# A two-block transformer step in float32 on one core: gates and return projection as seven token-major products, weight sums on GpSimd, last experts' blocks in halves

## What is computed

```python
# first block, cut to what matters; u_lat is the modulated input, 256 x 1024
q, k, v, g, glu, gates = split(u_lat @ w_in + b_in)          # g and gates: 2048 columns each
o = retention_in_both_directions(q, k, v, context)           # 256 x 2048, 8 heads
ret = silu(g) * head_norm(o)
y_a = ret @ w_ret_out                                        # 2048 -> 1024
z = depthwise_conv_31_taps(za * sigmoid(zb)) + b
z = silu(layernorm(z) * conv_g + conv_b)
y_b = z @ w_conv_out + b_conv_out
ga, gb = split(sigmoid(gates))
mix = (ga * y_a + gb * y_b) @ w_mix_out + b_mix_out
h = layernorm(ALPHA * h + gt_m * mix)
y = sum over 32 experts of combine[:, e] * ((silu(t @ w_gate[e]) * (t @ w_up[e])) @ w_down[e])
```

## Time and profile before

| | |
|---|---|
| median of three runs | 1438.39 us |
| the profiled execution | 1437.52 us, span 1435.7 us |
| TensorE (PE) busy | 1390.8 us, 97% |
| DVE busy | 611.6 us, 43% |
| ACT busy | 224.4 us, 16% |
| GpSimd busy | 18.1 us, 1% |
| read from HBM | 419 MB, mean 295 GB/s |
| granted TensorE clock, mean | 0.995 |

### The profile page before, as it was taken

How to read it: one execution, slowest core, us unless ns; L and a number is a source line. 1 busy time by engine, 2 the same in 40 slices (tenths; PEclk the granted TensorE clock), 3 DMA queues, 4 the chain that set the end, 5 groups by cost and what they waited for, 6 DMA issues and landing times.

```text
span 1435.7 us, 21518 instructions
## 1 busy us (share of the span) xinstructions
PE 1390.8 (97%) x9242; PEld 981.6 (68%) x9242; DVE 611.6 (43%) x1267; ACT 224.4 (16%) x445; POOL 18.1 (1%) x44
## 2 busy tenths in 40 slices
PE   9999999999999999999999999898999999999986
PEld 7888888678888887555545544444688887565543
DVE  1566899989883147222221122122512326122122
ACT  0211010321201104111011011011211203211001
POOL 0000000000000000000100000000100000000000
PEclk9999999999999999999999999999999999999999
DMA  9735231964344587999999999999443557899995
GB/s 383 317 146 81 81 132 66 350 244 191 128 165 157 211 344 317 398 415 427 409 426 425 426 425 427 425 425 428 157 188 152 219 207 293 311 385 423 426 424 233
DMA packets 36342, 423.05 MB, mean 295 GB/s; under 512 B 4352, under 2 KB 5768, under 8 KB 10776
## 3 DMA queue, kind: packets, MB, share of 16 engines
q1 hardware_dynamic: 33408, 415.33, 70.8%
q10 hardware_dynamic: 1176, 1.84, 1.1%
q0 software_dynamic: 1664, 4.52, 1.0%
HBM read 419.05 MB, written 2.62 MB: 294 GB/s over the span
## 4 chain that ended last, share of the span: by engine, by line
PE 76%; DMA 13%; DVE 9%; issue 1%; SPq 0%; ACT 0%; POOL 0%; DVEq 0%; POOLq 0%
PE PP L1004 21%; PE PP L1356 16%; PE PP L1393 8%; DMA KQ<-in_w_moe 5%; PE MB L1331 5%; DMA ZC<-in_w_moe 4%; PE PP L1160 3%; PE PP L1042 3%; DVE ZC L1698 2%; DMA ring<-in_w_moe 2%; PE PP L1074 2%; PE MB L1134 2%; PE PP L1365 2%; PE PP L1323 2%; DMA ring<-in_w_v 1%
## 5 line engine op out<-in xcount | busy, mean ns | idle before, releaser
L1004 PE MATMUL PP<-uT,ring 128*128 128x256 f32 x704 | 153.5, 379 | 0.0
L1004 PEld LDWEIGHTS PP<-uT,ring 128*128 128x128 f32 x704 | 133.3, 190 | 19.1 <-issue 1.1
L2248 DVE TENSOR_SCALAR wctx<-wctx 128x1 f32<-128x1 f32 x46 | 7.1, 153 | 265.7 <-PE PP L1356 219.6
L1698 DVE SCALAR_TENSOR_TENSOR ZC<-ZC,vec 128x256 f32<-128x256 f32 x240 | 116.2, 484 | 7.8
L1331 PE MATMUL MB<-V 64*128 64x512 f32 x336 | 93.8, 638 | 1.7 <-DVE V L2282 0.9
L1356 PE MATMUL PP<-ring,const 128*64 128x256 f32 x800 | 90.6, 380 | 3.0 <-DMA ring<-in_w_moe 2.9
L1356 PEld LDWEIGHTS PP<-ring,const 128*64 128x64 f32 x800 | 57.7, 137 | 37.8 <-issue 8.6
L2268 DVE SCALAR_TENSOR_TENSOR V<-V,wctx 128x256 f32<-128x256 f32 x84 | 40.7, 485 | 91.4 <-PE MB L1331 71.2
L824 ACT ACTIVATE V<-PP 128x256 f32<-128x256 f32 x42 | 16.2, 385 | 304.8 <-PE PP L1356 283.2
L1393 PE MATMUL PP<-ring,const 128*64 128x512 f32 x272 | 62.1, 598 | 0.0
L2282 DVE TENSOR_TENSOR V<-PP,uT 128x512 f32<-128x512 f32 x32 | 22.1, 692 | 82.3 <-PE PP L1393 82.3
(11 more groups left out here) (563 smaller groups left out, 2112.0 us busy)
## 6 DMA issues: line engine op xcount, KB each, us to landing
ring<-in_w_moe SPq DMA_DIRECT2D x51, 2048.0 KB, 16.8
RA<-in_w_moe SPq DMA_DIRECT2D x18, 2048.0 KB, 16.9
ZC<-in_w_moe SPq DMA_DIRECT2D x18, 2048.0 KB, 18.7
Vc<-in_w_moe SPq DMA_DIRECT2D x17, 2048.0 KB, 18.4
KQ<-in_w_moe SPq DMA_DIRECT2D x17, 2048.0 KB, 17.9
extra<-in_w_moe SPq DMA_DIRECT2D x17, 1792.0 KB, 15.0
ring<-in_w_ada SPq DMA_DIRECT2D x12, 2048.0 KB, 10.4
ring<-in_w_gates SPq DMA_DIRECT2D x7, 2048.0 KB, 7.7
```

The lines of the kernel that those rows point to most:

```text
L1004: ins = pe.matmul(out[:, c, :], W[:, k * width + at:k * width + at + P], X[:, k, :], start=k == 0, stop=k == K - 1)
L1698: ins = V_.scalar_tensor_tensor(conv[:, t, :], zpad[:, t, k:k + L], tap, conv[:, t, :], ALU.mult, ALU.add)
```

## The change

- **Gates and ret as seven products.** Gates (4 blocks) and ret (its 2048 x 1024 weight as two pairs of blocks, summed over two halves of the depth) go by the scheme of g, with token-major results: `token_products` (g and gates), `ret_products`. DVE adds the products into rows `gates_t` and `m_rows`.
- **Weight sums on GpSimd.** Of the five sums of a block, four go to GpSimd from the second g block on, two of the first; all ten of a pair of ret blocks too: 50 instructions of 128x1024. They have seven places in turn (`SUM_RING`). DVE keeps the fifth (and three of the first g block).
- **Mixed rows turned.** `cout` becomes a `tm8` job, the gating with gates is done on rows, and two pieces of 8 transposes (`turn_mixed`) bring the result to channel-major before `mix`.
- **Head norm** moves from DVE to ACT (16 instructions of 128x256, `Identity` with scale and bias).
- **Taps in turns.** Two channel tiles are convolved side by side: a tap waits for the one two before it (`own.follow`). Their places are dealt out anew, through g, gates and the first ret pair.
- **Last experts' blocks in halves.** Up comes as its first and last four k pieces, down as the two halves of every 512 columns (pieces of 1 KB a row); TensorE, DVE and the last scatter work by halves.
- **Bays.** The last ret block goes to RA, and the first nine expert blocks are loaded in another order; KQ is free once the mixed rows are turned, not when mix is done.

```diff
-FIRST_MOE0 = (2, 0, 1, 3, 8, 5, 7, 4, 6)
+FIRST_MOE0 = (2, 0, 6, 3, 8, 4, 1, 7, 5)
...
-                       ("k", 2, ["seven"]), ("v", 4, ["seven"]), ("ada", 8, ["ada"]), ("g", 4, ["seven"]), ("gates", 4, ["cm8"]),
-                       ("ret", 4, ["cm16"]), ("cout", 2, ["cm8"]), ("mix", 2, ["cm8"]))),
+                       ("k", 2, ["seven"]), ("v", 4, ["seven"]), ("ada", 8, ["ada"]), ("g", 4, ["seven"]), ("gates", 4, ["seven"]),
+                       ("ret", 4, ["ret"]), ("cout", 2, ["tm8"]), ("mix", 2, ["cm8"]))),
...
+        SUM_RING = [Eqb, Ddec, Pc, Ph, kw, Kc[:, 0:4, :], Kc[:, 4:8, :]]
...
+            def follow(self, ins):
+
+                self.n += 1
+                ins.then_inc(self.sem, 1)
+                self.eng.wait_ge(self.sem, self.n - 1)
...
+            def weight_sum(i, q, j=1):
+
+                w_wait(pool, J["ret", 2 * SEVEN[i][1] + j, 0]["w"] if i >= R7 else seven_job(i)["w"])
+                if G7 + 2 <= i < S7:
+                    seven_wait(pool, i - 2, 6)
+                if i >= S7:
+                    n = ring_place(i, q, j if i >= R7 else 0)
+                    if n >= len(SUM_RING):
+                        seven_wait(pool, *ring_user(n - len(SUM_RING)))
+                    elif n >= 4:
+                        seven_wait(pool, G7 + 2, 6)
+                x, y, op = weight_pair(*quarters(i, j))[q]
+                nc.gpsimd.tensor_tensor(sum_at(i, q, j if i >= R7 else 0), x, y, op).then_inc(pool_made, 1)
...
-                    t, k = step // TAPS, step % TAPS
+                    t, k = 2 * (step // (2 * TAPS)) + step % 2, step % (2 * TAPS) // 2
...
+            def ret_products(i, after_fourth=None):
+
+                for p in range(7):
+                    n = 7 * i + p
+                    pe.wait_ge(seven_kept, n - 3)
+                    for j in range(2):
...
+                        for k in range(4):
+                            ins = pe.matmul(gate_bank(n - 7 * G7), x[:, k, :], y[:, k, :], start=j == 0 and k == 0, stop=j == 1 and k == 3)
...
             for b in range(4):
                 for p in range(7):
-                    add_gate_product(b, p)
+                    add_token_product(G7 + b, p)
                     if p == 1 and b:
                         gate_ret(b - 1)
-                    if p > 1 and b < 3:
-                        add_weights(G7 + b + 1, p - 2)
-                    if p == 3:
-                        normalise(b)
+                    elif p < 6:
+                        taps(2 if p > 1 else 1)
+                    else:
+                        add_weights(G7 + b + 1, 4)
             gate_ret(3)
-            taps(DT * TAPS - tap_at[0])
+            for b in range(4):
+                for p in range(7):
+                    add_token_product(S7 + b, p)
+                    if b >= 2 and p < 5:
+                        ret_token_sum(b - 2, p)
+                    elif p == 6 and b < 3:
+                        add_weights(S7 + b + 1, 4)
+                    else:
+                        taps(2)
+            left = DT * TAPS - tap_at[0]
...
+            job(J["cout", 1, 0], at_half=lambda: turn_mixed(0))
...
                     pe.wait_ge(m["wg_full"], i * 16 + 16)
                     gate_or_up(0, wg, xs).then_inc(m["gate_done"], 1)
-                    pe.wait_ge(m["wu_full"], i * 16 + 16)
-                    gate_or_up(1, wu, xs).then_inc(m["up_done"], 1)
-                    pe.wait_ge(m["y_kept"], k + 1)
+                    up_halves(wu, i * 16 + 16).then_inc(m["up_done"], 1)
+                    pe.wait_ge(m["y_kept"], i * 2 + (WINDOWS[n] + 1))
...
+                    down_half(0, wd).then_inc(m["down_done"], 1)
+                    pe.wait_ge(m["wd_rest"], i * 16 + 16)
+                    down_half(1, wd).then_inc(m["down_done"], 1)
```

More of the change, by code:

```diff
@@ L172, in make_jobs @@
                 if src != "glu" or b == 3:
-                    loads.append(dict(src=src, b=b, bay=bay_of(phase)))
+                    loads.append(dict(src=src, b=b, bay=3 if (src, b) == ("ret", 3) else bay_of(phase)))
         experts(n)
@@ L404, in build @@
                                           "rooted", "u_scaled", "u2_scaled", "res", "gate_ps", "gate_kept")}
-        fin = {k: sem(f"fin_{k}") for k in ("row", "divided", "scaled", "rows")}
+        fin = {k: sem(f"fin_{k}") for k in ("divided", "scaled", "rows")}
         def out_wait(eng):
@@ L441, in seven_job @@
         def seven_job(i):
-            return J[SEVEN[i][0], SEVEN[i][1], 0]
+            src, b = SEVEN[i]
+            return J[src, 2 * b + 1 if src == "ret" else b, 0]
         def seven_wait(eng, i, p):
@@ L530, in last_experts @@
                     for q in range(3):
-                        sp.wait_ge(m[PARTS[q][1]], i + 1)
-                        sp.dma_start(bays[own[q]], s[bass.ds(3 * e + q, 1)].rearrange("a p n -> p (a n)")
-                                     ).then_inc(m[PARTS[q][0]], 16)
+                        sp.wait_ge(m[PARTS[q][2]], i * 2 + 1 if q == 2 else i + 1)
+                        into, block = bays[own[q]], s[bass.ds(3 * e + q, 1)].rearrange("a p n -> p (a n)")
+                        if q == 0:
+                            sp.dma_start(into, block).then_inc(m[PARTS[q][0]], 16)
+                            continue
+                        for half in range(2):
+                            if q == 1:
+                                part = lambda x: x[:, half * 2048:(half + 1) * 2048]
+                            else:
+                                part = lambda x: x.rearrange("p (c h n) -> p c h n", h=2, n=L)[:, :, half, :]
+                            sp.dma_start(part(into), part(block)).then_inc(m[PARTS[q][half]], 16)
             at = [first_of_moe[0]["w"], J["u2", 0, 0]["w"], first_of_moe[1]["w"], len(loads)]
@@ L614, in _, with bias_row @@
             pool.dma_start(outside, a["outside"]).then_inc(b2["ld"], 16)
-            for n in range(8):
+            def bias_row(n):
                 if n >= 2:
@@ L746, in turned_copy @@
                 ins.then_inc(ret_kept, 1)
+            act.wait_ge(var_ready, 2)
             for b in range(4):
+                for h in (2 * b, 2 * b + 1):
+                    for t in range(LT):
+                        o = On[:, t, h * DV:(h + 1) * DV]
+                        nc.scalar.activation(o, o, ACT.Identity, scale=rstd[:, t * HEADS + h:t * HEADS + h + 1], bias=mv[:, t, h, 1:2])
                 act.wait_ge(seven_kept, 7 * (G7 + b + 1))
@@ L753, in _ @@
             for b in range(4):
-                j = J["gates", b, 0]
-                job_wait(act, j)
-                for i in range(4):
-                    ins = nc.scalar.activation(gT[:, 4 * b + i, :], PP[j["pair"]][:, i, :], ACT.Sigmoid,
-                                               bias=col("b_gates", 4 * b + i))
-                ins.then_inc(pair_free[j["pair"]], 1)
+                act.wait_ge(seven_kept, 7 * (S7 + b + 1))
+                gate = gates_t[:, :, 512 * b:512 * (b + 1)]
+                nc.scalar.activation(gate, gate, ACT.Sigmoid).then_inc(g_silu, 1)
             for half in range(2):
@@ L772, in _ @@
                 ln_say(act, ins, out, 1)
+            for half in range(2):
+                act.wait_ge(ret_turned, 5 + half)
+                for q in range(2):
+                    ins = nc.scalar.activation(m_first[:, 4 * half + 2 * q:4 * half + 2 * q + 2, :], MB[2 * half + q][:, :, :], ACT.Copy)
+                ins.then_inc(ret_kept, 1)
             def route_and_experts(n):
@@ L981, in _, with job @@
         def _(pe):
-            def job(j, tiles=None, between=None):
+            def job(j, tiles=None, between=None, at_half=None):
                 w_wait(pe, j["w"])
@@ L1011, in job @@
                 elif kind in ("tm8", "tm8c"):
-                    X = ucT if kind == "tm8c" else uT
+                    X = conv if j["src"] == "cout" else uT
                     for t in range(LT):
+                        if t and at_half is not None:
+                            at_half()
                         for k in range(DT):
@@ L1152, in gate_products @@
                         w_wait(pe, seven_job(i)["w"])
-                    pe.wait_ge(sums_made, sums)
+                    if i == G7 and sums is not None:
+                        pe.wait_ge(sums_made, 5 * G7 + sums)
+                    if p >= 2:
+                        sums_ready(pe, i, y)
+                        y = sum_at(i, y)
                     if n >= 7 * G7 + 4:
@@ L1699, in convolve @@
                     if step < DT * TAPS - 1:
-                        link(ins)
+                        own.follow(ins)
                     else:
@@ L1803, in _ @@
                     else:
[L1804 removed]
+                        taps((2, 2, 2, 2, 2, 4)[i] if (i, p) != (5, 6) else 0)
                 if i in (2, 3):
@@ L1831, in _ @@
                     decay(h + 2)
-                taps(4 if h < 7 else 0)
+                taps(5 if h < 7 else 0)
                 if h:
```

(2 more changed lines are left out.)

324 lines of the change are left out of this document (213 added, 111 removed).

## The result

| | before | after |
|---|---|---|
| median | 1437.93 us (4 runs, 1437.22 to 1441.15) | 1481.86 us (4 runs, 1480.88 to 1482.01) |
| profiled execution, span | 1435.7 us | 1479.1 us |
| busy: PE, DVE, POOL | 1390.8, 611.6, 18.1 us | 1391.2, 687.3, 151.0 us |

The ratio is 1.0298, with a 95% interval of 1.0286 to 1.031: slower by 3%. I had forecast 1421.0, with 1414 to 1460 as range. The prediction was wrong, in sign and in range.

A forecast was written before the change was run, and what follows sets the result against it. TensorE's matmul count bounds g, gates and ret, and the weight stream follows PE's start: gates -6.9, ret -6.9, turns +1.8 (net -12.0) and experts' ends -5.4 give -17.4 us, so 1421.0 us, range 1414 to 1460.

The forecast's parts named there:

- What covers it: In g, gates and ret: GpSimd's sums, DVE's additions and taps, and ACT's head norm cost nothing, hidden beside other work.
- Rival 1: From g to ret, GpSimd sums and DVE taps exclude each other: stage 42 us later, 1463 us; chance 0.22.
- Gates 12.08 us a block, 6.9 us less: Gates: four jobs of 13.81 us become four blocks of 12.08 us, 6.9 us less.
- Ret 6.9 us less: Ret: 4 x 64 = 256 matmuls become 2 x 112, 6.9 us less.
- Turns 1.8 us, cout at nothing: Before mix: two pieces of eight transposes add 1.8 us of PE; token-major cout costs nothing and waits hide.
- A sum on GpSimd 2.45 us: In g, gates and ret: each 1024-element sum takes GpSimd 2.45 us, fifty of them 122 us.
- rival 2: In gates and ret, GpSimd sums are slower than its one row says: 1430 us at 3.0 us each; chance 0.15.
- A pair of taps 0.91 us: DVE in g and gates: two taps taken in turns cost 0.91 us together.
- The 10.7 us for 26 taps of the first ret pair: DVE in the first ret pair: 26 taps take 10.7 us, part of 19.3 of 24.2 us.
- Tails 5.4 us: Last experts' blocks in halves at both experts' ends: 2.7 us less for each, 5.4 in all.
- The last scatter's half beside DVE: At the experts' ends: half of the last scatter is done beside DVE's last part, some 0.5 us.
- The experts' stream moves with PE's start: First block's experts: bays tie the weight stream to PE's start, so the end moves by the same time.

The follow-up runs named there:

- experiments 3 and 5: 3: changed kernel without 91 of its 93 taps, 1433.15 us; 5: all weight sums on DVE, 40 taps earlier, 1443.09 us, then also ret in full, 1428.80 us.
- experiment 1: Kernel before, plus 45 idle GpSimd sums of 1024 elements that nobody needs: 1504.21 us, ratio 1.046.
- experiment 6: Against the run with early taps and ret in full (1428.80 us), GpSimd again makes four of five sums of g and gates blocks: 1428.66 us, ratio 0.9926.

## Why the prediction was wrong

**The step that failed** is "What covers it", with its words "This sum costs three things at nothing, each by work beside it". GpSimd's sums and DVE's taps are not beside each other. I added up each engine apart (10.3 us of GpSimd, 11.5 of DVE, against 13.0), where the sum of those parts of both that exclude each other had to be held against 13.0. Rival 1 did that: 16.8 us for a g block, and 16.8 was measured. The match is in part luck. By its own terms (4 x 2.45 + 1.22 + 1.23 + 9 x 0.485) g comes to 16.6. In the block shown above the four sums took 10.9 us, in which the excluding lengths of both engines add up to 12.5, so the hold-off is a little less than the full lengths; and in the 5.9 us without a sum DVE spent some 2 on additions, which this count leaves out. Rival 1 had a chance of 0.22, "because the rule is only a page's here". What spoke for it (DVE at 88 and 96% by my own count) said how dear it would be if true; what spoke against it was the absence of rows, which is no evidence. As its time lay 42 us away on the wrong side, the range of 1460 also cut off the case.

**Rival 1's own size** was short by 19 us (1463). g is right, gates too (65.6 against 2 x 16.8 and two lighter blocks). The first ret pair was put at 37 us and took 52.2. Three things were missing. In ret, sums stand back to back, so taps and sums take turns, and six taps took 14.92 us where my sum gave them 0.485 each. Tiny instructions pay the full wait: the four of 128x8 below took 9.7 us, and with them PE's wait of 8.26 us. And PE had half the clock for a while after these gaps: behind the one of 8.26 us, eight instructions took 3.57 us (466.14 to 469.71), where they take 1.73 at full clock; the mean is 0.85 from 475.9 to 521.5.

```profile
454.73 2.32 DVE L1811 TENSOR_SCALAR modT<-modT 128x8 f32<-128x8 f32 x1
457.09 2.26 DVE L1813 TENSOR_TENSOR fold<-vec,modT 128x8 f32<-128x8 f32 x1
459.38 2.26 DVE L1814 TENSOR_TENSOR fold<-vec,modT 128x8 f32<-128x8 f32 x1
461.68 2.85 DVE L1815 TENSOR_TENSOR fold<-fold,modT 128x8 f32<-128x8 f32 x1
```

**Step by step, the rest.**
- *Gates 12.08 us a block, 6.9 us less*: right, 12.09 in experiments 3 and 5.
- *Ret 6.9 us less*: PE's count was right (24.2 us for the products of the second pair with taps gone; all of ret in 49.5 us for 55.9 with 40 taps gone). What failed is DVE's side: with ret's token sums, its weight sums and the remaining taps, g and gates took 118.6 us, and the kernel was 5 us slower than before.
- *Turns 1.8 us, cout at nothing*: right, 1.6 in all, and no turn stalled.
- *A sum on GpSimd 2.45 us*: right, 2.5 alone; rival 2 is out.
- *A pair of taps 0.91 us*: right, 0.88 where nothing excludes. Their turns alone are worth nothing, since TensorE was full. The 10.7 us for 26 taps of the first ret pair go by 0.41 each and not by the pair, which would give 11.8; eight in a row took 3.26 us there, so 0.41 was the better price.
- *Tails 5.4 us*: mis-sized, 3.6. "half of up (1.8 us) is done before the landing, so down starts 1.8 us sooner" overlooked that TensorE is still at gate when the first half of up lands. What can go is the time between gate's end and up's start, 1.4 us where up came whole. Up's landing is the first line of the earlier trace rows. The last scatter's half beside DVE, put at some 0.5 us, and DVE's shorter copy leave about 0.5 together.
- *The experts' stream moves with PE's start*: right, the first expert job started 47.2 us later than before (597.73 for 550.51) and the last gate job of that block 47.25 (1033.88 for 986.63); its row statistics came 45.3 later (1048.62 for 1003.30), which leaves 1.9 for the tail.

What stays open: why a `tensor_scalar` is held through several memsets in two cases and through one in a third, and whether the taps dealt out anew, without ret in full, would have been enough. In experiment 1 I had allowed 50 us and 66 were lost; I know where, but I had no sum that gives the 37.67 us of the one long wait.

## What to carry to other kernels

Before work is moved to GpSimd, list for each block the instructions of both engines by what they read. Those of GpSimd that read SBUF and those of DVE with two SBUF inputs (and, here, `tensor_scalar` ones of one SBUF tensor too: 1036 ns for 409 in the head norm of experiment 1) add up to one column, and that column has to fit in the block of the engine that bounds; DVE's reads of PSUM stay outside it. The column is an estimate: it was near in g (16.6 for 16.8 us) and held in experiment 6, but was too low in ret and in the run with 22 sums on GpSimd, where DVE waits in its order. Where DVE itself bounds, a sum of 1.22 us on DVE that becomes 2.45 us of both is a loss, and holes of DVE in earlier stages are the better place to look: 40 taps moved into them are worth 12 us, and g starts no later for it (315.11 for 315.26 us).

## What the hardware showed that I had not expected

- The hold-off reaches to the end of the other's instruction and works in both directions, and it asks nothing of size: a 128x8 instruction waited 2.3 us, a sum of DVE 3.3 us beside one of GpSimd that itself grew from 2.5 to 3.3.
- GpSimd's memsets (128x1024 in 0.90 us each) leave a tap (485 ns) and DVE's sums (1.22 us) as they are, yet a 128x16 `tensor_scalar` took 6.43 us, until the last of twelve was done, and a 128x256 one 4.40 us; a 128x8 one passed after 0.88 us, with more memsets to come.
- Additions with one PSUM and one SBUF input never changed: 411 to 425 ns as a mean of each group, in every trace of this stage.
